# A streaming encoder layer on one core: the heads' turn in 194 finer steps, with two state buffers and a new order

## The reference, cut to what matters

```python
# group A, per head: masked logits -> softmax -> values -> times silu(z)
logits = q k^T * scale - slope * |t - s|      # positions outside the top-k: -inf
o_a = softmax(logits) v * silu(z_a)
# group B, per head: causal conv (width 4) + silu on q, k, v; L2-normalised q, k; per block of tokens
decay = exp(gc_i - gc_j); a_mat = strict_lower(k b k^T * decay)
u, w = solve(I + a_mat, [v b, k b exp(gc)])   # unit lower triangular
v_new = u - w s                               # s: 128 x 128 state, block after block
o = (q exp(gc)) s + (q k^T * decay) v_new
s = s * exp(g_last) + (k exp(g_last - gc))^T v_new
o_b = rmsnorm(o) * silu(z_b)
y = rmsnorm(x + [o_a, o_b] w_out)
```

## Time and profile before

| | |
|---|---|
| runs | 3172.86, 3158.35, 3160.65 us; median 3160.65 |
| profiled execution | 3176.13 us, span 3174.0 us, granted TensorE clock 0.921 |
| busy share of the span | TensorE 88%, VectorE 36%, ScalarE 30%, GpSimd 26% |
| the heads | from 1826.5 to 2652.5 us, 826 us of the span |
| the turn used below | turn 2, from 2148.8 us (first `D_turn` of head 3) to 2244.3 us (first `D_turn` of head 4) |

### The profile page before, as it was taken

The page is one execution under the profiler, slowest core; times in us unless marked ns, Lnnn a source line. Parts: engine busy times, 40 slices in busy tenths (PEclk is TensorE's granted clock), DMA queues, the critical chain, the costliest instruction groups (busy, mean ns, idle before and its releaser), DMA issues. The chain is left out here.

```text
span 3174.0 us, 40095 instructions
## 1 busy us (share of the span) xinstructions
PE 2804.9 (88%) x15405; PEld 2516.8 (79%) x15429; DVE 1156.2 (36%) x2044; ACT 948.0 (30%) x1657; POOL 819.6 (26%) x713
## 2 busy tenths in 40 slices
PE   4999899999999999999999747787788785799997
PEld 3999599798998989999999736666677663587875
DVE  7000100752909044070600154566665552204142
ACT  5111111313112121121211245555556542222221
POOL 6222022111111211211122212323312320355553
PEclk6999699999999989999999877988998995699998
DMA  3222222122121212212222321222122113446453
GB/s 127 64 72 63 42 62 66 55 65 65 59 75 45 68 49 65 81 49 67 66 65 70 110 84 40 78 78 70 28 67 70 56 42 85 169 153 228 159 179 126
DMA packets 301721, 259.04 MB, mean 82 GB/s; under 512 B 88232, under 2 KB 252176, under 8 KB 299152
## 3 DMA queue, kind: packets, MB, share of 16 engines
q1 hardware_dynamic: 291564, 212.35, 23.0%
q10 hardware_dynamic: 10048, 45.27, 3.5%
HBM read 192.25 MB, written 65.33 MB: 81 GB/s over the span
## 5 line engine op out<-in xcount | busy, mean ns | idle before, releaser
L394 PE MATMUL bank<-hH,wL 128*128 128x384 f32 (+1 forms) x2928 | 981.5, 335 | 14.9 <-POOL wL L311 14.9
L395 PE MATMUL bank<-hL,wH 128*128 128x384 f32 (+1 forms) x2928 | 979.9, 335 | 0.0
L396 PE MATMUL bank<-hH,wH 128*128 128x384 f32 (+1 forms) x2928 | 979.7, 335 | 0.0
L311 POOL TENSOR_TENSOR wL<-raw,wH 128x512 fp32r<-128x512 f32 x244 | 314.2, 1288 | 1388.7 <-ACT wH L328 1388.7
L394 PEld LDWEIGHTS bank<-hH,wL 128*128 128x128 f32 (+1 forms) x2928 | 549.8, 188 | 19.2 <-issue 18.5
L395 PEld LDWEIGHTS bank<-hL,wH 128*128 128x128 f32 (+1 forms) x2928 | 549.9, 188 | 0.8
L396 PEld LDWEIGHTS bank<-hH,wH 128*128 128x128 f32 (+1 forms) x2928 | 549.8, 188 | 0.7
L328 ACT ACTIVATE wH<-raw 128x512 fp32r<-128x512 f32 x244 | 154.2, 632 | 1018.9 <-PE bank L396 963.1
L1906 POOL TENSOR_TENSOR owL<-oraw,owH 128x2048 fp32r<-128x2048 f32 x48 | 225.5, 4700 | 267.7 <-ACT owH L1926 267.7
L506 DVE TENSOR_SCALAR score<-relued,w_idx 128x512 f32<-128x512 f32 (+3 forms) x10 | 7.8, 778 | 683.4 <-ACT relued L353 683.0
L1965 PE MATMUL ob<-owH,mL 128*128 128x512 f32 x576 | 227.0, 394 | 28.6 <-POOL owL L1906 28.6
(11 more groups left out here) (302 smaller groups left out, 3521.0 us busy)
## 6 DMA issues: line engine op xcount, KB each, us to landing
raw<-in_w_in SPq DMA_DIRECT2D x240, 256.0 KB, 2.8
oraw<-in_w_out SPq DMA_DIRECT2D x48, 1024.0 KB, 5.1
proj_scratch<-ptbuf ACTq DMA_DIRECT2D x60, 576.0 KB, 2.8
xc<-proj_scratch SPq DMA_DIRECT2D x8, 1536.0 KB, 7.6
mraw<-mix_scratch SPq DMA_DIRECT2D x12, 768.0 KB, 6.1
x<-in_x_prompt SPq DMA_DIRECT2D x8, 1024.0 KB, 4.9
out_y_prompt<-yv ACTq DMA_DIRECT2D x8, 1024.0 KB, 4.4
ox<-in_x_prompt SPq DMA_DIRECT2D x8, 768.0 KB, 6.8
```

Of the source, the lines that this page charges most:

```text
L311: pool.tensor_tensor(wL[c % 2][:, :, :], raw[c][:, :, :], wH[c % 2][:, :, :].bitcast(F32), ALU.subtract).then_inc(low_ready, 1)
L394: pe.matmul(o, low, hH[:, kk, tok], start=first, stop=False)
L395: pe.matmul(o, high, hL[:, kk, tok], start=False, stop=False)
L396: last = pe.matmul(o, high, hH[:, kk, tok], start=False, stop=end)
```

## The change

It has three parts.

**Finer steps.** `D_gram` becomes `D_decay` and `D_gram`, which no longer carry each other's neighbour; `D_level` becomes `D_level_w` and `D_level_z`; `D_last` becomes `D_last_x` and `D_last_z`; `S_out` gives its two halves of the states' update to `S_update`; `O_norm` becomes `O_sum`, `O_norm` and `O_scale`; the output part of `M_read` and `M_state` (q times the state, the second part, the scaling and the addition) becomes `M_out`. The instructions stay the same in number and shape.

**Two buffers.** `S` and `vn` are two each, used by the parity of t. VectorE's subtraction of tile t now waits for the output products of tile t-2 instead of t-1, and the state's update for those of tile t-1.

**A new order.** The rules of `iteration` give way to a table `TURN` of 194 steps, each with the head's distance (0, 1, 2 or 3) from the turn's number; line numbers below 760 stay, later ones fall by about 30 to 45.

```diff
--- before.py
+++ after.py
@@ -757,73 +757,42 @@
-def iteration(i):
...
-        placed += spread(0.0, 0.42, states) + spread(0.42, 0.50, sample) + spread(0.50, 0.62, out)
-        placed += spread(0.56, 0.80, levels) + spread(0.80, 0.86, [("D_last", h, q) for q in range(3)]) + spread(0.88, 0.98, solves)
-        placed += spread(0.62, 0.80, natural) + spread(0.80, 0.95, norms)
...
+TURN = [
+    ("A_exp", 1, 0), ("A_logits", 1, 0), ("A_bias", 1, 0), ("A_logits", 1, 1), ("D_out", 1, 0), ("D_turn", 1, 0), ("D_turn", 1, 1), ("D_turn", 1, 2),
...
+        order += [(name, i + ahead, k) for name, ahead, k in TURN if 0 <= i + ahead < H]
-        S = sbt("S", [P, P])
+        S = [sbt(f"S{i}", [P, P]) for i in range(2)]
         Ss = sbt("Ss", [P, DEC_B, P])
-        vn = sbt("vn", [P, P])
+        vn = [sbt(f"vn{i}", [P, P]) for i in range(2)]
         vn_sample = uw[:, NT, 1, :]
...
+                def level_w(h, s):
+                    lo, hi = PAIRS5[LEVEL_STEPS[s][1]]
+                    wait(act, wt_done, h, s + 1)
+                    if s >= 2:
+                        wait(act, z_done, h, s - 1)
+                    else:
+                        wait(act, last_done, h - 1, 2)
+                    copy(WT[s % 2][:, 0:hi - lo, :], quad(w_bank(s))[:, 0:hi - lo, :]).then_inc(wt_ready.sem, 1)
...
+                def decay(h, p):
+                    lo, hi = PAIRS5[p]
+                    if p == 0:
+                        wait(pe, qk_ready, h, 5)
+                    if p >= 2:
+                        wait(pe, decay_ready, h, p - 1)
...
+                    last.then_inc(cum_done.sem, 1)
+
                 def gram(h, p):
-                    halves = pair_slots(h)
-                    if p < 5:
...
-                    if p >= 1:
-                        lo, hi = PAIRS5[p - 1]
...
+                    lo, hi = PAIRS5[p]
+                    if p == 0:
+                        wait(pe, qk_ready, h, 5)
+                    else:
+                        wait(pe, a_ready, h, p)
+                    for t in range(lo, hi):
+                        last = pe.matmul(big[:, D_BANK + 2, (t - lo) * 2 * P:(t - lo + 1) * 2 * P], qkT[:, 1, t, :], qkT[:, pair_slots(h), t, :], start=True, stop=True)
+                    last.then_inc(gram_done.sem, 1)
+
...
+                def level_z(h, s):
+                    m, g = LEVEL_STEPS[s]
+                    lo, hi = PAIRS5[g]
+                    wait(pe, wt_ready, h, s + 1)
+                    if s == NS - 1:
+                        wait(pe, tu_ready, h, s - 1)
+                    for t in range(lo, hi):
+                        z = big[:, z_bank(s), (t - lo) * 2 * P:(t - lo + 1) * 2 * P]
+                        pe.matmul(z[:, 0:P], WT[s % 2][:, t - lo, :], TU[:, t, 0, :], start=True, stop=True)
+                        last = pe.matmul(z[:, P:2 * P], TU[:, t, 0, :], WT[s % 2][:, t - lo, :], start=True, stop=True)
+                    last.then_inc(z_done.sem, 1)
...
-                    pe.matmul(big[:, 0, 0:P], uw[:, t, 1, :], S[:, :], start=True, stop=True).then_inc(ws_done.sem, 1)
+                    pe.matmul(big[:, 0, 0:P], uw[:, t, 1, :], S[t % 2][:, :], start=True, stop=True).then_inc(ws_done.sem, 1)
+
+                def state(h, t):
+
+                    wait(pe, vn_ready, h, t + 1)
+                    pe.matmul(big[:, 0, P:2 * P], kd[h % 2][:, t, :], vn[t % 2][:, :], start=True, stop=True).then_inc(ds_done.sem, 1)
+
+                def state_out(h, t):
+                    wait(pe, vn_ready, h, t + 1)
                     if t:
                         wait(pe, o_ready, h, t)
-                    pe.matmul(big[:, 1, 0:P], qkT[:, q_slot(h), t, :], S[:, :], start=True, stop=True)
-
-                def state(h, t):
-
-                    wait(pe, vn_ready, h, t + 1)
-                    pe.matmul(big[:, 0, P:2 * P], kd[h % 2][:, t, :], vn[:, :], start=True, stop=True).then_inc(ds_done.sem, 1)
-                    pe.matmul(big[:, 1, P:2 * P], AQ[:, q_slot(h), t, :], vn[:, :], start=True, stop=True).then_inc(oo_done.sem, 1)
+                    pe.matmul(big[:, 1, 0:P], qkT[:, q_slot(h), t, :], S[t % 2][:, :], start=True, stop=True)
+                    pe.matmul(big[:, 1, P:2 * P], AQ[:, q_slot(h), t, :], vn[t % 2][:, :], start=True, stop=True).then_inc(oo_done.sem, 1)
...
+                def sample_update(h, half):
                     wait(pe, sm_mask, h, 1)
                     wait(pe, o_ready, h, TILES)
...
+                    for b in range(4):
+                        last = pe.matmul(big[:, half, b * P:(b + 1) * P], kd_seg[:, 4 * half + b, :], vn_sample, start=True, stop=True)
+                    last.then_inc(sm_ds.sem, 1)
...
-                        V.memset(S[:, :], 0.0).then_inc(state_zero.sem, 1)
+                        V.memset(S[0][:, :], 0.0).then_inc(state_zero.sem, 1)
                         wait(dve, uw_ready, h, 5)
                     wait(dve, ws_done, h, t + 1)
-                    if t:
-
-                        wait(dve, oo_done, h, t)
-                    V.tensor_tensor(vn[:, :], uw[:, t, 0, :], big[:, 0, 0:P], ALU.subtract).then_inc(vn_ready.sem, 1)
+                    if t >= 2:
+
+                        wait(dve, oo_done, h, t - 1)
+                    V.tensor_tensor(vn[t % 2][:, :], uw[:, t, 0, :], big[:, 0, 0:P], ALU.subtract).then_inc(vn_ready.sem, 1)
 
                 def state(h, t):
                     wait(dve, ds_done, h, t + 1)
-                    V.scalar_tensor_tensor(out=S[:, :], in0=S[:, :], scalar=K["egl"][:, h, t:t + 1], in1=big[:, 0, P:2 * P], op0=ALU.mult, op1=ALU.add).then_inc(s_ready.sem, 1)
+                    if t:
+                        wait(dve, oo_done, h, t)
+                    V.scalar_tensor_tensor(out=S[(t + 1) % 2][:, :], in0=S[t % 2][:, :], scalar=K["egl"][:, h, t:t + 1], in1=big[:, 0, P:2 * P], op0=ALU.mult, op1=ALU.add).then_inc(s_ready.sem, 1)
+
+                def add_out(h, t):
...
+                def out_sum(h, _k):
                     wait(dve, o_squares, h, 1)
                     V.tensor_reduce(osq[:, 0, :], kd_seg[:, :, :], AX_X, ALU.add).then_inc(o_norms.sem, 1)
...
+                def out_scale(h, _k):```

What the new order does at three places. On **TensorE**, between the samples' update (`kd_seg`), the output's transpositions (`ident,uw`) and the first levels (`TU,Bm` is w; `TU,WT` and `WT,TU` are z), turn 2 had:

```order
L1384 MATMUL big<-uw,kd_seg 128x128 x8
L1424 MATMUL big<-PT,keep_vN 128x128 x6
L1395 MATMUL big<-ident,uw 128x128 x4
L1295 MATMUL big<-TU,Bm 128x128 x2
L1405 MATMUL big<-keep_mask,keep_identb 128x512
L1406 MATMUL big<-keep_kT,qa 128x512
L1395 MATMUL big<-ident,uw 128x128 x4
L1418 MATMUL big<-ident,lg 128x128 x4
L1295 MATMUL big<-TU,Bm 128x128 x2
L1306 MATMUL big<-TU,WT 128x128
L1307 MATMUL big<-WT,TU 128x128
```

More of the change, by code:

```diff
@@ L757, in upto @@
         return h * self.per + k
-def spread(first, last, steps):
-    return [(first + (last - first) * (i + 0.5) / len(steps), step) for i, step in enumerate(steps)]
-def iteration(i):
[L767 to L774, removed]
-        placed += spread(0.0, 0.42, states) + spread(0.42, 0.50, sample) + spread(0.50, 0.62, out)
[L776 to L783, removed]
-        placed += spread(0.56, 0.80, levels) + spread(0.80, 0.86, [("D_last", h, q) for q in range(3)]) + spread(0.88, 0.98, solves)
[L785 to L812, removed]
-        placed += spread(0.62, 0.80, natural) + spread(0.80, 0.95, norms)
[L814 to L820, removed]
@@ L1122, in decay @@
                 def decay(h, p):
-                    if p == 5:
-                        return
                     lo, hi = PAIRS5[p]
@@ L1217, in _ @@
                 run({"N_tap": tap, "N_silu": silu, "N_tails": tails, "N_turn": natural, "N_squares": head_squares, "N_norms": root,
-                     "D_turn": qk_out, "D_gram": decay, "D_level": level, "D_last": last_level, "D_solve": solve, "M_state": state, "S_state": sample_state, "S_new": sample_new,
+                     "D_turn": qk_out, "D_decay": decay, "D_level_w": level_w, "D_last_x": last_x, "D_solve": solve, "M_out": state, "S_state": sample_state, "S_new": sample_new,
                      "O_square": square, "O_norm": out_root, "A_silu": gate_a, "O_silu": gate_b, "A_exp": exps, "A_turn_p": p_out})
@@ L1425, in values @@
                     last.then_inc(pv_done.sem, 1)
-                run({"N_tails": tails, "N_turn": natural, "D_turn": qk_turn, "D_gram": gram, "D_level": level, "D_last": last_level, "D_solve": solve,
-                     "M_read": read, "M_state": state, "S_state": sample_state, "S_turn": sample_turn, "S_out": sample_out, "O_out": out,
+                run({"N_tails": tails, "N_turn": natural, "D_turn": qk_turn, "D_decay": decay, "D_gram": gram, "D_level_w": level_w, "D_level_z": level_z, "D_last_x": last_x, "D_last_z": last_z, "D_solve": solve,
```

(1 more changed line is left out.)

199 lines of the change are left out of this document (90 added, 109 removed).

## The result

| | before | after |
|---|---|---|
| median of the runs of one session (us) | 3166.76 (3158.35 to 3184.45) | 3067.76 (3065.55 to 3071.7) |
| profiled execution: span, granted clock | 3174.0, 0.921 | 3066.2, 0.937 |
| the turn with heads 0 and 1, from the first `D_turn` | 1867.3 to 1958.4 | 1868.1 to 1945.3 |
| the six full turns | 570.4 | 485.3 |
| end of the heads | 2652.5 | 2551.6 |

The ratio is 0.967, 95% interval 0.9649 to 0.9691: 3.3% faster; the forecast was 3077. Of the 107.8 us of the span, 13.9 come from the turn with heads 0 and 1, 85.1 from the six full turns, 13.3 from the turn without convolution; the last turn gives 10.6 back; 6.9 lie behind the heads, 0.8 are lost ahead of them.

What follows compares the result with a forecast made beforehand. A loop through PSUM banks 2 to 4 was taken to fill each turn: 25 + 30 + 29 = 84 us instead of 95.1. Six turns 66.6, two others 10 and 7: 3160.65 - 83.6 = 3077 us, range 3035 to 3135.

Steps and rivals of the forecast that it cites:

- Piece a: Turn's start to the last product in `AQ`; forecast 25 us instead of 27.0, bounds 20 and 29.
- `N_pads` then ends at 10.1: Piece a: VectorE's copy of 72 columns, held by GpSimd's run, ends 10.1 us into the turn instead of 7.5.
- the copy gets in earlier: Rival, 0.12: `N_pads` ends near 4.2, transposed keys on ScalarE limit piece a to 20.5; 3050 us.
- Piece b: Last product to first level's matmul, the blocks' trip through memory and GpSimd; forecast 30.0 us, bounds 28 and 33.
- none of it touched: Piece b: the change leaves the trip's 29.8 us, first store to last load into `TU`, as they were.
- Piece c: First level's matmul to next turn; 29 us, bounds 25 and 34; first half, to last `N_turn`, 19.5, second 9.8.
- The wait at the root: Piece c, first half: third copy of w on ScalarE stands behind the outputs' root; TensorE waits 2.6 us.
- The double buffers: Two `S` and `vn`, with the split of M: cost nothing by themselves; loop over banks 0 and 1 stays hidden.
- The other turns: Heads 0 and 1 turn: 91.1 to 81; without convolution: 81.3 to 74; first and last turn: nothing.
- Slower: Rival, 0.06: levels wait through the root for VectorE's 27 us in piece b; turn 105, 3220 us.
- nothing comes of it: Rival, 0.08: the loop over banks 0 and 1 is the true limit; turn stays at 95, 3160 us.
- the root eats half: Rival, 0.15: root's chain comes 6 us later, levels from the third on with it; turn 90, 3124 us.

Runs made afterwards that it cites:

- e5: Changed kernel, with GpSimd's three scalings of keys and values waiting for `O_scale` of the head before; 3049.7 us.
- e8: Changed kernel, with two taps and two exponentials put back between the decays on ScalarE; 3070.5 us.
- e9: Changed kernel, with two logits, one set of attention weights and two sets of values put back between the decays on TensorE; 3087.2 us.
- e11: Changed kernel with the edits of e8 and e9 together; 3115.0 us.
- e3: Changed kernel, with no convolutions beside the base on GpSimd: four straight behind the last product, three behind `S_update`; 3113.5 us.
- e10: On top of e5: second level's products wait for `O_norm`, two more convolutions ahead of the base, last two behind `S_update` and `O_norm`; 3029.7 us.
- e4: Changed kernel, with two logits, two sets of values and four sets of transpositions of attention weights put back among the levels; 3139.2 us.
- e1: Changed kernel with one `S` and one `vn` instead of two, all `M_out` straight behind `M_state`; 3083.8 us.
- e12: On top of e10: seventh convolution moved behind `S_update`, eighth behind `O_norm`, ninth behind the first level's update; 3039.6 us.
- e2: Changed kernel, with GpSimd's three scalings of keys and values waiting for the last product in `AQ`; 3057.1 us.
- e6: On top of e5: four of the eight loads into `TU` issued by ScalarE instead of SyncE; 3046.6 us.

## Why the prediction was right, step by step

**Piece a: 25 forecast, 20.1 measured, the low bound.** The step that failed: "`N_pads` then ends at 10.1". It ended at 6.3, since VectorE was let in behind the third of GpSimd's scalings, and the sign named for it, `N_pads` of 6 to 8 us, was 2.13. The prediction took the run as one block up to the clearing. In the kernel before, the six long copies came beside the third scaling and had the clearing next; the short one came beside the third scaling too (2247.84), so no row told ahead of time which it would be. In the changed kernel `S_keys` stands next, and ahead of it the copy was let in in all six full turns. What decides this no run shows. The rival "the copy gets in earlier" had the early end, if at 4.2, and its sum for piece a, 20.5, was right; its reason was not. It named the transposed keys on ScalarE as the limit, but e5 shows 15.7 once GpSimd's run is gone: three held steps of VectorE were the limit, 4.4 us. From the end of `N_pads` to the last product, 15 were forecast and 13.8 measured. That gain is a joint one of ScalarE's and TensorE's lists (e8, e9, e11); the prediction gave ScalarE's rows as its main ground, and these alone are worth nothing.

**Piece b: 30 forecast, 32.5 measured.** The mechanism was right: the trip is the longest, w waits for the load in all eight heads, TensorE's own work (24.9 us in turn 2, 25.6 forecast) was done 7.8 us before. Mis-sized was "none of it touched". The trip's base went from 14.2 to 15.4 us with three or four convolutions beside it to 17.5 to 18.8 with five, and a sixth at its end; with none it is 11.8 (the turn without convolution) or 11.6 (e3), with two 13.3 to 14.6 (e10). The seven convolutions were counted as VectorE's time, and not as GpSimd's. The Trainium skill (SBUF — State Buffer, "Who interferes with whom") says that a VectorE instruction with two inputs in SBUF contends with a GpSimd instruction that reads SBUF; a convolution is of that kind, and the trace agrees, 1.46 us for a step of 0.26. Worked out afterwards: a convolution costs the base (17.7 - 11.6) / 5 = 1.2 us, two more beside it make the trip 29.8 + 2.4 = 32.2.

**Piece c: 29 forecast, 28.3 measured.** Its main term, 9.0 us of TensorE taken out of the levels, is shown by e4 (9.2). The second half was 9.7 (9.8 forecast), and the 2.6 us of waiting for the solve went to 0.1, as forecast. The wait at the root, 2.6 forecast, did not come: `O_norm` ended 31.5 to 33.4 us after the last product, about when w began (31.4 to 33.6, later than forecast), so the root ran while TensorE had two z to do. In its place stands a slower clock. TensorE over its wait, the first 3.2 us after it, and on (columns of the earlier trace rows):

```profile
2150.20:2158.00 7.80, 0.07 (x1) 0.00 (x0) 7.80 (x6) 0.00 (x0) 4.37 (x4) 0.76 0.33 46
2158.00:2161.20 3.20, 3.14 (x15) 3.14 (x16) 0.50 (x3) 1.39 (x3) 0.00 (x0) 0.53 0.87 306
2161.20:2172.00 10.80, 10.68 (x96) 10.42 (x96) 8.09 (x13) 9.38 (x18) 0.00 (x0) 1.00 0.61 173
```

After 7.8 us without work the clock is 0.53, near the lower level of 1.2 GHz, for 3.2 us: an estimated 3.2 x 0.47 = 1.5 us lost. In e1, where w waits for nothing in five of the six full turns, the same 3.2 us of turn 2 run at full speed:

```profile
2165.24:2168.44 3.20, 3.17 (x29) 2.98 (x28) 2.99 (x7) 2.46 (x5) 0.00 (x0) 1.00 0.72 230
```

In those five turns the first half is 16.6 us (16.9 forecast without the root's wait) and piece c 26.4, against 18.5 and 28.3: 1.9 us. The root itself is the limit only where the trip is shorter: in e10 and e12.

**The double buffers: nothing forecast, about 1 us per turn measured** (e1), through the place at which VectorE meets GpSimd's products.

**The other turns.** Turn -1 gained 13.9 (10 forecast), the turn without convolution 13.3 (7). For the last turn nothing was forecast; it lost 10.6, at a clock of 0.57 in its first half where the old one had 0.91. The traces part this: e4, e8 and e10, whose last turn has the same steps in the same order, pass it in 46.5 to 46.9 us with 0.88 to 0.91 in the first half. So some 6 of the 10.6 go with the clock and 4 with the new order; why the clock fell there is not shown. Nor is shown why 6.9 us went behind the heads: in all thirteen other traces, that of before among them, this part takes 520.7 to 523.7 us, here 514.6.

**The sum.** a, b and c were off by -4.9, +2.5 and -0.7: errors of both signs, so the turn of 84 became 80.9. That the time came within 10 us of 3077 is luck in part. The gain was 99.0 us between the medians, 107.8 between the traces, and not 83.6; the last turn's loss took some of it back, and the kernel before, 3160.65 in the forecast's sum, had 3166.76 as the median of the session. "Slower" and "nothing comes of it" did not occur; "the root eats half" has its place in e10, not here.

## What to carry to other kernels

When a table moves VectorE's steps about, read beside each of them what GpSimd does at that moment: the same instruction cost 0.2, 2.1 or 4.1 us here, and it lengthened GpSimd's in turn. A step moved out of such a run helps only if it does not meet the next one (e2, e3 and e12 moved the collision, e5 avoided it, e10 in part). Where two engines' lists both feed a chain, undo them one by one and together: alone they cost -0.2 and 1.2 us of a turn here, together 4.5.

## What the runs showed of the hardware

- VectorE's held steps were let in at the end of one of GpSimd's three scalings (2.03 and 2.13 us), but not between the keys of the samples and the clearing (2.52 us, to the end of the clearing), and not between the four products of 1.23 us each (6.72 us, to the end of the last). By the Trainium skill (SBUF — State Buffer, "Who interferes with whom") whoever issues first holds the shared pair for one whole instruction; the first two agree, the last two do not. Ahead of the clearing six of the seven copies of the kernel before were held too, 4.06 us.
- Eight loads take 3.8 us to issue on one queue, four and four on two queues 1.9 (e6); the last one then landed 0.5 us later after its issue, so w came 1.3 us earlier and not 1.9.
